# Block inverses of the gated DeltaNet mixer: 32x32 diagonal blocks for four levels, the last level as single 32x32 products

## The chip, the cores and the metric

One NeuronCore of a Trainium2 chip runs the whole layer in one launch. The time is the device time of one execution in microseconds (us), given as the median of several executions. TensorE (PE) multiplies, VectorE (DVE) and ScalarE (ACT) do element-wise work and empty PSUM, GpSimd (POOL) and SyncE (SP) mostly start transfers. A matmul of 32-bit floats shows in the trace as two MATMUL records and two weight loads (LDWEIGHTS, engine PEld), so 16 matmuls are 32 records.

## The reference, cut to what matters

The layer is a half-step SwiGLU network, a token mixer and a second SwiGLU network. Half of the mixer is a gated DeltaNet with 8 heads in both directions, in chunks of 64 tokens. For every chunk it solves a unit lower triangular 64x64 system:

```python
def gdn_chunked(q, k, v, beta, g, h0):
    ...
    kk = jnp.einsum('bhnck,bhnmk->bhncm', k, k)
    a_mat = eye + jnp.where(pos[:, None] > pos[None, :], beta[..., :, None] * decay * kk, 0.0)
    rhs = jnp.concatenate([beta[..., None] * v, (beta * gamma)[..., None] * k], axis=-1)
    sol = lax.linalg.triangular_solve(a_mat, rhs, left_side=True, lower=True, unit_diagonal=True)
    ...
    def step(h, xc):
        u = vt_c - jnp.einsum('bhck,bhkv->bhcv', w_c, h)
        o = jnp.einsum('bhck,bhkv->bhcv', qg_c, h) + jnp.einsum('bhcm,bhmv->bhcv', pqk_c, u)
        h = h * gl_c[..., None, None] + jnp.einsum('bhck,bhcv->bhkv', kd_c, u)
        return h, o
```

The 256 context and 256 latent tokens are 8 chunks per head and direction. The other half of the mixer is a 2-D Fourier transform ("fnet" in the code).

## The kernel before, in words

Before and after the mixer the kernel runs large projections: TensorE multiplies weight tiles that ACT and DVE split into two parts each (`parts`). The change touches none of this.

The mixer is a loop written out by hand, `for i in range(-1, HEADS + 1)`, once for each engine: `mixer_pe`, `mixer_dve`, `mixer_act`. In iteration i three heads are in work: head i+1 (`a`) gets its decays and its chunk matrix, head i (`m`) gets its inverse, head i-1 (`b`) runs its scan over the 8 steps. Every engine executes its instructions in the order written; semaphores (`hs[...]`, counted per head by `PER`) tie the engines together. Iteration 0 also carries the Fourier half.

All 8 chunks of a head stand side by side in one tile of 128 partitions by 512 columns: partitions 0 to 63 hold the forward direction, 64 to 127 the backward one, and each chunk has 64 columns. The inverse S of (I + N) is built by doubling the size of the diagonal blocks, from 2 to 64. `start_S` makes the first S (the 2x2 blocks) out of `n_T` with two DVE instructions, `start_T` transposes it into `g_T`. Each of the five levels is then a chain through two engines:

- PE `y_level`: `n_T` (stationary) times `g_T` (moving), 8 chunks x 2 halves = 16 matmuls into bank B_Y
- DVE `level_Y`: times the mask `LEVEL[lv]`, out to `g_Y`
- PE `x_level`: `g_Y` (stationary) times `g_S` (moving), 16 matmuls into bank B_X
- DVE `level_S`: `g_S` minus the product
- DVE `level_T`: `g_T` is the transpose of `g_S` (not after the last level)

```python
for s in range(STEPS):
    last = pair_mm(B_Y, CHUNK * s, n_T[:, m.h % 2, s, :], g_T[:, m.h % 2, s, :])
```

`pair_mm` issues one 64x64 matmul for the upper and one for the lower partitions. `DVE transpose` works within 32x32 blocks. After level 4 (the fifth) PE runs `solve_w` and `solve_v`, which multiply S with `kbg` and `vb`.

Between the products of the levels stand the scan of head b (`scan_read` s on PE, `scan_u` s on DVE, `scan_write` s on PE, `scan_state` s on DVE, in that circle) and, for head m, transposes of keys and values (`token_k`, `token_v`). ACT is in the loop for `decays` (`dT`), `values` (`vb`), `w_out_of` (`wT`), `vt_out_of` (`vt`) and the output norm. In the last iterations the output projection starts: `split_out` on ACT and DVE and `out_products` on PE.

## Time and profile before

| | |
|---|---|
| median of 3 runs | 3061.83 us (3061.67 to 3066.12) |
| profiled execution, its own time | 3063.91 us |
| its span in the trace | 3062.1 us |
| busy: PE, PEld, DVE, ACT, POOL | 97%, 80%, 59%, 31%, 1% of the span |
| granted TensorE clock, mean | 0.991 |
| mixer loop in the trace | from about 1912 us to about 2226 us |
| from the first level product of head 1 to that of head 7 | 1959.43 to 2160.04 us, six heads |

The profile's page gives shares over the whole span, which the large projections fill. The mixer is a tenth of it; what bounds it has to be read from the timeline of each engine in one head's iteration and from the chain of waits there. A MATMUL's time in a timeline row runs to its modelled end; from the start of one row to the start of the next is the time that the products take in a stream.

### The profile page before, as it was taken

To read this page: it belongs to the slowest core of one execution; us is meant where nothing else is said; L and a number is where in the kernel's file an instruction comes from. 1 tells how busy PE (TensorE), PEld (TensorE's weight loads), DVE (VectorE), ACT (ScalarE), POOL (GpSimd) and SP (SyncE) were. 2 spreads that over 40 slices of the span, in tenths; PEclk is the share of its full clock that TensorE was granted. 3 is DMA by queue.
4 is the path that set the end of the run, shared out by engine and by line. 5 is a ranking of instruction groups with operands and counts; after the bars stand their busy time and mean duration, and the time that the engine had idled before them with its cause. 6 is when DMAs were issued, how large, how long until landed. Compare 5 with 4: busy or idle time off the path is not lost. (4 is left out here: it accounts for less than half of the span.)

```text
span 3062.1 us, 43016 instructions
## 1 busy us (share of the span) xinstructions
PE 2959.7 (97%) x17705; PEld 2444.6 (80%) x17705; DVE 1814.1 (59%) x2027; ACT 949.2 (31%) x1155; POOL 25.3 (1%) x35
## 2 busy tenths in 40 slices
PE   6899999999999999999979999999999999999998
PEld 3688888888888888888868899777777888888887
DVE  3346565665565656565674566667556655666666
ACT  3222221221222222221352356211245343434333
POOL 0000000000000000000000000000000000000000
PEclk9999999999999999999989999999999999999999
DMA  9726444454544557575723354000254555555553
GB/s 370 267 96 206 137 165 152 151 180 136 194 147 155 202 211 261 182 271 202 291 64 105 97 168 141 10 9 9 92 185 165 182 189 192 179 190 179 192 191 124
DMA packets 307694, 508.07 MB, mean 166 GB/s; under 512 B 8252, under 2 KB 230020, under 8 KB 291684
## 3 DMA queue, kind: packets, MB, share of 16 engines
q1 hardware_dynamic: 305312, 496.83, 48.0%
q0 software_dynamic: 1408, 8.86, 0.8%
q8 instruction: 112, 1.84, 0.3%
q10 hardware_dynamic: 836, 0.33, 0.0%
q14 instruction: 26, 0.21, 0.0%
HBM read 503.85 MB, written 2.15 MB: 165 GB/s over the span
## 5 line engine op out<-in xcount | busy, mean ns | idle before, releaser
L2182 PE MATMUL ps<-xn,parts 128*128 128x512 f32 (+1 forms) x8992 | 1788.9, 361 | 6.6 <-DVE parts L1471 3.2
L2182 PEld LDWEIGHTS ps<-xn,parts 128*128 128x128 f32 x8992 | 1515.7, 189 | 277.7 <-issue 6.8
L1471 DVE TENSOR_TENSOR parts<-raw,parts 128x1024 fp32r<-128x1024 f32 x632 | 755.9, 1221 | 412.6 <-ACT parts L828 412.3
L828 ACT ACTIVATE parts<-raw 128x1024 fp32r<-128x1024 f32 x634 | 656.2, 1055 | 1093.3 <-PE ps L2182 890.3
L2182 PE MATMUL ps<-parts,h_parts 128*128 128x512 f32 x3168 | 729.8, 390 | 1.6 <-DVE h_f L1516 1.5
L2182 PEld LDWEIGHTS ps<-parts,h_parts 128*128 128x128 f32 x3168 | 591.5, 188 | 135.5 <-issue 6.1
L1504 DVE SCALAR_TENSOR_TENSOR macc<-raw,cs,macc 128x2048 f32<-128x2048 f32 x150 | 348.1, 2346 | 0.0
L1606 DVE TENSOR_TENSOR acc<-acc,ps 128x512 f32<-128x512 f32 x160 | 110.0, 688 | 212.4 <-PE ps L2182 212.4
L866 ACT ACTIVATE h_parts<-h_f 128x512 fp32r<-128x512 f32 (+1 forms) x42 | 35.1, 836 | 356.2 <-DVE h_f L1563 356.2
L1563 DVE TENSOR_TENSOR h_f<-silu_g,ps 128x1024 f32<-128x1024 f32 x20 | 24.4, 1222 | 146.0 <-PE ps L2182 146.0
L2182 PE MATMUL ps<-parts,xn 128*128 128x512 f32 x384 | 91.6, 394 | 0.0
L2182 PEld LDWEIGHTS ps<-parts,xn 128*128 128x128 f32 x384 | 71.0, 188 | 15.1 <-issue 0.5
L1598 DVE TENSOR_TENSOR acc<-acc,ps 128x1024 f32<-128x1024 f32 x42 | 51.3, 1221 | 35.3 <-PE ps L2182 32.4
L1557 DVE TENSOR_REDUCE h_f<-ps 128x512 f32<-128x1024 f32 x22 | 27.0, 1226 | 73.3 <-PE ps L2182 73.3
L1551 DVE TENSOR_REDUCE silu_g<-ps 128x512 f32<-128x1024 f32 x22 | 27.0, 1226 | 72.3 <-PE ps L2182 72.3
L1796 DVE SCALAR_TENSOR_TENSOR cv<-ps,convT,cv 128x248 f32<-128x248 f32 (+3 forms) x160 | 66.1, 472 | 0.1
L1565 DVE TENSOR_TENSOR h_parts<-h_f,h_parts 128x512 fp32r<-128x512 f32 (+1 forms) x42 | 39.8, 947 | 37.9 <-ACT h_parts L866 37.9
L1896 PE MATMUL ps<-g_T,n_T 64*64 64x64 f32 x1280 | 45.9, 221 | 2.6 <-DVE g_T L1224 1.7
L1896 PEld LDWEIGHTS ps<-g_T,n_T 64*64 64x64 f32 x1280 | 40.4, 134 | 8.2 <-DVE g_T L1224 6.0
L1896 PE MATMUL ps<-g_S,g_Y 64*64 64x64 f32 x1280 | 45.9, 221 | 1.0 <-DVE g_Y L1218 0.2
L1896 PEld LDWEIGHTS ps<-g_S,g_Y 64*64 64x64 f32 x1280 | 40.4, 134 | 7.2 <-DVE g_Y L1218 4.5
L2182 PE MATMUL ps<-raw,cpad 128*32 128x512 f32 x160 | 25.0, 715 | 18.6 <-DMA raw<-in_w_mod 18.6
(239 smaller groups left out, 1205.8 us busy)
## 6 DMA issues: line engine op xcount, KB each, us to landing
raw<-in_w_mod SPq DMA_DIRECT2D x132, 1024.0 KB, 5.4
raw<-in_w_up SPq DMA_DIRECT2D x88, 1024.0 KB, 5.1
raw<-in_w_down SPq DMA_DIRECT2D x88, 1024.0 KB, 5.3
raw<-in_w_gate SPq DMA_DIRECT2D x84, 1024.0 KB, 5.1
raw<-in_w_in SPq DMA_DIRECT2D x41, 1024.0 KB, 5.3
raw<-in_w_out SPq DMA_DIRECT2D x16, 1024.0 KB, 5.1
extra<-in_w_mod SPq DMA_DIRECT2D x12, 1024.0 KB, 14.3
gate_raw<-in_w_gate SPq DMA_DIRECT2D x4, 1024.0 KB, 14.2
```

Of the source, the lines that this page charges most:

```text
L828: nc.scalar.activation(parts[:, unit % PART_SLOTS, 0, :], raw[:, slot, b * UNIT:(b + 1) * UNIT], ACT.Copy).then_inc(hi_ready, 1)
L866: nc.scalar.activation(gpart[:, 0, 2 * s:2 * s + 2, :], h_f32[:, :, 0:N], ACT.Copy).then_inc(h_hi, 1)
L1471: nc.vector.tensor_tensor(parts[:, pslot, 1, :], raw[:, slot, b * UNIT:(b + 1) * UNIT], parts[:, pslot, 0, :].bitcast(F32), ALU.subtract)\
L1504: ins = nc.vector.scalar_tensor_tensor(macc[:, s, :], raw[:, slot, :], cs[:, k, s:s + 1], macc[:, s, :], ALU.mult, ALU.add)
L1551: nc.vector.tensor_reduce(silu_g[:, :, 0:N], halves(4 * s), axis=mybir.AxisListType.X, op=ALU.add).then_inc(g_sum, 1)
L1557: nc.vector.tensor_reduce(h_f32[:, :, 0:N], halves(up), axis=mybir.AxisListType.X, op=ALU.add).then_inc(u_sum, 1)
L1565: nc.vector.tensor_tensor(gpart[:, 1, 2 * s:2 * s + 2, :], h_f32[:, :, 0:N], gpart[:, 0, 2 * s:2 * s + 2, :].bitcast(F32), ALU.subtract)\
L1598: nc.vector.tensor_tensor(a[:, :, cols], a[:, :, cols], ps[:, bank:bank + 2, :], ALU.add).then_inc(down_added, 1)
L1606: nc.vector.tensor_tensor(a[:, t, cols], a[:, t, cols], ps[:, down_bank(tiles, j, t), :], ALU.add).then_inc(down_added, 1)
L1796: nc.vector.scalar_tensor_tensor(o, s_, tap, o, ALU.mult, ALU.add).then_inc(conv_op, 1)
L1896: return nc.tensor.matmul(o, lhsT, rhs, start=start, stop=stop)
L2182: return nc.tensor.matmul(o, lhsT, rhs, start=start, stop=stop)
```

## The change

S is kept compact while its diagonal blocks are at most 32 wide: `c_S` and `c_T` hold 32 columns per chunk (256 in all) where `g_S` and `g_T` held 64 (512 in all). Two ACT instructions per head, `diagonal_blocks`, copy `n_T` into `n_D` and zero the off-diagonal 32x32 blocks by a per-partition scale of 0 or 1 (`SIDE`). `start_S` becomes three DVE instructions of 256 columns. In levels 0 to 3 the products stay 16 matmuls each with the same 64x64 stationary operand, and move 32 columns instead of 64; `level_Y` still writes 512 columns, `level_S` and `level_T` handle 256. `inverse_blocks`, two ACT instructions, spreads `c_S` into the full `g_S` (now one buffer). The last level is built apart: `outer_y` and `outer_x` are 16 matmuls each with a stationary operand of 32x32, ACT copies the product between them (`outer_Y`), and the result goes into `g_S` by one ACT instruction (`outer_forward`) and one DVE instruction (`outer_backward`) on 32 partitions each. The constants shrink from 10 to 8 small masks.

```diff
@@ -232,12 +241,14 @@
...
-        g_T = ra("g_T", [P, 2, STEPS, CHUNK])
-        g_S = ra("g_S", [P, 2, STEPS, CHUNK])
+        c_T = ra("c_T", [P, 2, STEPS, BLOCK])
+        c_S = ra("c_S", [P, 2, STEPS, BLOCK])
+        g_S = ra("g_S", [P, STEPS, CHUNK])
+        g_Y = ra("g_Y", [P, STEPS, CHUNK])
         c2 = sb("c2", [P, C2_COLS], R_RAW + 3 * slot_bytes)
         rp = Bump(R_PARTS, R_PARTS + slot_bytes)
         n_T = rp("n_T", [P, 2, STEPS, CHUNK])
-        g_Y = rp("g_Y", [P, STEPS, CHUNK])
+        n_D = rp("n_D", [P, 2, STEPS, CHUNK])
         rp = Bump(R_PARTS + slot_bytes, R_PARTS + 2 * slot_bytes)
         kbg = rp("kbg", [P, STEPS, P])
         vb = rp("vb", [P, STEPS, P])
@@ -434,14 +454,14 @@
 
         PER = {
 
-            "gm_ok": 1, "e_mm": 1, "e_exp": 1, "kk_mm": 1, "sb_ok": 1, "ib_ok": 1, "n_half": 1, "n_ok": 1,
-            "t_init": 1, "s_half": 1, "s_init": 1,
+            "gm_ok": 1, "e_mm": 1, "e_exp": 1, "kk_mm": 1, "sb_ok": 1, "ib_ok": 1, "n_half": 1, "n_ok": 1, "nd_ok": 2,
+            "t_init": 1, "s_init": 3,
 
             "kT": 2, "kd_ok": 2, "kbg_ok": 2, "vT": 2, "vb_ok": 2, "qg_ok": 1,
             "qk_mm": 1, "p_half": 1, "p_ok": 3, "f_a": 1, "f_mid_ok": 1, "f_b": 1, "f_even": 1, "f_v": 2, "f_hi": 1,
             "f_lo": 1,
 
-            "y_mm": 5, "y_ok": 5, "x_mm": 5, "t_ok": 4, "s_ok": 5, "w_mm": 1, "w_ok": 2, "vt_mm": 2,
+            "y_mm": 5, "y_ok": 5, "x_mm": 5, "t_ok": 4, "s_ok": 4, "S_ok": 4, "w_mm": 1, "w_ok": 2, "vt_mm": 2,
             "vt_ok": 2,
 
             "wh_mm": 7, "u_ok": 7, "dh_mm": 7, "st_ok": 13, "oT_mm": 1, "osq": 1, "oss_mm": 1, "oss_ln": 1,
@@ -689,6 +709,30 @@
                 a.ago(2, "n_half", "p_half")
                 nc.scalar.activation(flat(dT[:, a.h % 2]), ps[:, B_A, :], ACT.Exp).then_inc(hs["e_exp"], 1)
 
+            def diagonal_blocks(a):
+                a.wait("n_ok")
+                a.ago(2, "y_mm", "s_init")
+                for e, cols in enumerate(SIDES):
+                    nc.scalar.activation(n_D[:, a.h % 2, :, cols], n_T[:, a.h % 2, :, cols], ACT.Copy, scale=SIDE[e])\
+                        .then_inc(hs["nd_ok"], 1)
+
+            def inverse_blocks(m):
+                m.wait("s_ok")
+                m.last("vt_mm")
+                for e, cols in enumerate(SIDES):
+                    nc.scalar.activation(g_S[:, :, cols], c_S[:, m.h % 2], ACT.Copy, scale=SIDE[e])\
+                        .then_inc(hs["S_ok"], 1)
+
+            def outer_Y(m):
+                m.wait("y_mm")
+                nc.scalar.activation(y_off, blocks(B_Y), ACT.Copy).then_inc(hs["y_ok"], 1)
+
+            def outer_forward(m):
+                m.wait("x_mm")
+                m.wait("S_ok", 2)
+                nc.scalar.activation(g_S[Q0, :, SIDES[1]], blocks(B_X, Q0), ACT.Copy, scale=-1.0)\
+                    .then_inc(hs["S_ok"], 1)
+
             def values(m, g):
                 m.wait("vT", g + 1)
                 m.last("vt_mm")
@@ -763,6 +807,8 @@
                     out_root(was)
                 if not m and a:
                     fnet_mid(fn[0])
+                if a:
+                    diagonal_blocks(a)
                 if first:
                     fnet_between(1)
                     fnet_between(2)
@@ -785,13 +831,19 @@
                     values(m, 1)
                     if first:
                         fnet_mid(fn[6])
+                    inverse_blocks(m)
+                    outer_Y(m)
+                    if first:
                         fnet_between(6)
+                    if i < HEADS - 1:
+                        outer_forward(m)
                 if i == HEADS - 1:
                     act.wait_ge(hs["qg_ok"], HEADS)
                     act.wait_ge(hs["p_ok"], HEADS * PER["p_ok"])
                     act.wait_ge(hs["e_mm"], HEADS)
                     act.wait_ge(hs["n_ok"], HEADS)
                     split_out(0)
+                    outer_forward(m)
                     split_out(1)
                 if i == HEADS:
                     act.wait_ge(hs["x_mm"], HEADS * PER["x_mm"])
@@ -1192,15 +1244,17 @@
 
             def start_T(a):
                 a.wait("s_init")
-                nc.vector.transpose(flat(g_T[:, a.h % 2]), flat(g_S[:, a.h % 2])).then_inc(hs["t_init"], 1)
+                nc.vector.transpose(flat(c_T[:, a.h % 2]), flat(c_S[:, a.h % 2])).then_inc(hs["t_init"], 1)
 
             def start_S(a):
-                a.wait("n_ok")
+                a.wait("nd_ok")
                 a.ago(2, "vt_mm")
-                S = g_S[:, a.h % 2]
-                nc.vector.tensor_tensor(S, n_T[:, a.h % 2], every(M1T), ALU.mult).then_inc(hs["s_half"], 1)
-                a.wait("s_half")
-                nc.vector.tensor_tensor(S, every(PAIR_ID), S, ALU.subtract).then_inc(hs["s_init"], 1)
+                S, D = c_S[:, a.h % 2], n_D[:, a.h % 2]
+                nc.vector.tensor_tensor(S, D[:, :, SIDES[0]], D[:, :, SIDES[1]], ALU.add).then_inc(hs["s_init"], 1)
+                a.wait("s_init", 1)
+                nc.vector.tensor_tensor(S, S, every(OWN_M1T), ALU.mult).then_inc(hs["s_init"], 1)
+                a.wait("s_init", 2)
+                nc.vector.tensor_tensor(S, every(OWN_ID), S, ALU.subtract).then_inc(hs["s_init"], 1)
 
             def token_k(m, g, part):
                 src = ps[:, (B_A, B_B)[g], :].rearrange("p (s c) -> p s c", s=4)
@@ -1215,13 +1269,16 @@
 
             def level_Y(m, lv):
                 m.wait("y_mm", lv + 1)
-                nc.vector.tensor_tensor(g_Y[:], ps[:, B_Y, :].rearrange("p (s c) -> p s c", c=CHUNK), every(LEVEL[lv]),
+                two = [P, STEPS, 2, BLOCK]
+                nc.vector.tensor_tensor(g_Y[:].rearrange("p s (e c) -> p s e c", e=2),
+                                        blocks(B_Y).unsqueeze(2).to_broadcast(two),
+                                        LEVEL[lv].rearrange("p (e c) -> p e c", e=2).unsqueeze(1).to_broadcast(two),
                                         ALU.mult).then_inc(hs["y_ok"], 1)
 
             def level_T(m, lv):
 
                 m.wait("s_ok", lv + 1)
-                nc.vector.transpose(flat(g_T[:, m.h % 2]), flat(g_S[:, m.h % 2])).then_inc(hs["t_ok"], 1)
+                nc.vector.transpose(flat(c_T[:, m.h % 2]), flat(c_S[:, m.h % 2])).then_inc(hs["t_ok"], 1)
 
             def level_S(m, lv):
                 m.wait("x_mm", lv + 1)
@@ -1229,8 +1286,14 @@
                     m.wait("s_ok", lv)
                 else:
                     m.wait("s_init")
-                S = flat(g_S[:, m.h % 2])
-                nc.vector.tensor_tensor(S, S, ps[:, B_X, :], ALU.subtract).then_inc(hs["s_ok"], 1)
+                S = flat(c_S[:, m.h % 2])
+                nc.vector.tensor_tensor(S, S, ps[:, B_X, 0:STEPS * BLOCK], ALU.subtract).then_inc(hs["s_ok"], 1)
+
+            def outer_backward(m):
+                m.wait("x_mm")
+                m.wait("S_ok", 2)
+                nc.vector.tensor_scalar(g_S[Q3, :, SIDES[0]], blocks(B_X, Q3), -1.0, None, ALU.mult)\
+                    .then_inc(hs["S_ok"], 1)
 
             def query_gates(m):
                 m.eng.wait_ge(gam_in[m.h % 2], 16 * (m.h // 2 + 1))
@@ -1430,7 +1493,6 @@
                 if i == HEADS - 1:
                     query_matrix(m)
 
-                level_Y(m, 4)
                 if b:
                     scan_u(b, 7)
                 if i + 2 < HEADS:
@@ -1438,7 +1500,7 @@
                 if first:
                     fnet_out(fn[6])
                     fnet_lo(fn[6])
-                level_S(m, 4)
+                outer_backward(m)
                 if i < HEADS - 1:
                     query_half(m)
                     query_matrix(m)
@@ -1976,9 +2038,9 @@
                 else:
                     m.wait("t_init")
                     m.last("vt_ok")
-                    m.wait("n_ok")
+                    m.wait("nd_ok")
                 for s in range(STEPS):
-                    last = pair_mm(B_Y, CHUNK * s, n_T[:, m.h % 2, s, :], g_T[:, m.h % 2, s, :])
+                    last = pair_mm(B_Y, BLOCK * s, n_D[:, m.h % 2, s, :], c_T[:, m.h % 2, s, :], BLOCK)
                 inc(last, "y_mm")
 
             def x_level(m, lv):
@@ -1988,19 +2050,37 @@
                 else:
                     m.wait("s_init")
                 for s in range(STEPS):
-                    last = pair_mm(B_X, CHUNK * s, g_Y[:, s, :], g_S[:, m.h % 2, s, :])
+                    last = pair_mm(B_X, BLOCK * s, g_Y[:, s, :], c_S[:, m.h % 2, s, :], BLOCK)
                 inc(last, "x_mm")
 
+            def outer_y(m):
+                m.wait("t_ok")
+                m.wait("y_ok", LEVELS)
+                m.wait("n_ok")
+                for s in range(STEPS):
+                    cols = slice(BLOCK * s, BLOCK * s + BLOCK)
+                    mm(ps[Q1, B_Y, cols], n_T[Q0, m.h % 2, s, SIDES[1]], c_T[Q0, m.h % 2, s, :])
+                    last = mm(ps[Q2, B_Y, cols], n_T[Q3, m.h % 2, s, SIDES[0]], c_T[Q3, m.h % 2, s, :])
+                inc(last, "y_mm")
+
+            def outer_x(m):
+                m.wait("y_ok")
+                m.wait("s_ok")
+                for s in range(STEPS):
+                    cols = slice(BLOCK * s, BLOCK * s + BLOCK)
+                    mm(ps[Q0, B_X, cols], y_off[Q1, s, :], c_S[Q1, m.h % 2, s, :])
+                    last = mm(ps[Q3, B_X, cols], y_off[Q2, s, :], c_S[Q2, m.h % 2, s, :])
+                inc(last, "x_mm")
+
             def solve_w(m):
 
-                m.wait("s_ok")
-                m.wait("t_ok")
+                m.wait("S_ok")
                 m.wait("kbg_ok")
                 for s in range(STEPS):
                     for half, c_ in enumerate((s, high_block(back(s)))):
                         rows = HALVES[half]
                         last = mm(ps[:, B_XT + half, CHUNK * s:CHUNK * s + CHUNK], kbg[rows, c_, :],
-                                  g_S[rows, m.h % 2, c_, :])
+                                  g_S[rows, c_, :])
                 inc(last, "w_mm")
 
             def solve_v(m, g):
@@ -2156,13 +2236,13 @@
                 if b:
                     scan_write(b, 6)
 
-                y_level(m, 4)
+                outer_y(m)
                 if b:
                     scan_read(b, 7)
                 if first:
                     fnet_positions(fn[6])
                     fnet_channels(fn[7])
-                x_level(m, 4)
+                outer_x(m)
                 if b:
                     scan_write(b, 7)
                 if first:
```

On DVE, in the iteration of a middle head, from the second level on, the order before is (g_Y, g_S, g_T are `level_Y`, `level_S`, `level_T`; u_buf and st the scan):

```order
849 L1288 SCALAR_TENSOR_TENSOR st<-st,sc_all,ps 128x128 x2
850 L1233 TENSOR_TENSOR g_S<-g_S,ps 128x512
851 L1277 TENSOR_TENSOR u_buf<-vt,ps 128x128
852 L1224 STREAM_TRANSPOSE g_T<-g_S 128x512
853 L1288 SCALAR_TENSOR_TENSOR st<-st,sc_all,ps 128x128 x2
854 L1300 TENSOR_TENSOR o_out<-o_out,qzf 128x256
855 L1218 TENSOR_TENSOR g_Y<-ps,c_108 128x512
856 L1277 TENSOR_TENSOR u_buf<-vt,ps 128x128
857 L1201 TENSOR_TENSOR g_S<-n_T,early 128x512
858 L1203 TENSOR_TENSOR g_S<-early,g_S 128x512
859 L1233 TENSOR_TENSOR g_S<-g_S,ps 128x512
```

and now:

```order
850 L1351 SCALAR_TENSOR_TENSOR st<-st,sc_all,ps 128x128 x2
851 L1290 TENSOR_TENSOR c_S<-c_S,ps 128x256
852 L1340 TENSOR_TENSOR u_buf<-vt,ps 128x128
853 L1281 STREAM_TRANSPOSE c_T<-c_S 128x256
854 L1351 SCALAR_TENSOR_TENSOR st<-st,sc_all,ps 128x128 x2
855 L1363 TENSOR_TENSOR o_out<-o_out,qzf 128x256
856 L1273 TENSOR_TENSOR g_Y<-ps,c_110 128x512
857 L1340 TENSOR_TENSOR u_buf<-vt,ps 128x128
858 L1253 TENSOR_TENSOR c_S<-n_D 128x256
859 L1255 TENSOR_TENSOR c_S<-c_S,early 128x256
860 L1257 TENSOR_TENSOR c_S<-early,c_S 128x256
861 L1290 TENSOR_TENSOR c_S<-c_S,ps 128x256
```

The order is the same but for the third instruction of `start_S`; the subtractions and transposes have half the columns, the masked copies to g_Y have not.

On ACT, one middle head before:

```order
448 L690 ACTIVATE dT<-ps 128x512
449 L733 ACTIVATE r_o<-ps,ssq 128x256
450 L736 ACTIVATE r_o<-r_o 128x256
451 L740 ACTIVATE xn_52<-o_out 128x256
452 L695 ACTIVATE vb<-ps 128x512 x2
453 L728 ACTIVATE sq_o<-ps 128x256
454 L716 ACTIVATE wT<-ps 128x8x64 x2
```

and now:

```order
458 L710 ACTIVATE dT<-ps 128x512
459 L777 ACTIVATE r_o<-ps,ssq 128x256
460 L780 ACTIVATE r_o<-r_o 128x256
461 L716 ACTIVATE n_D<-n_T,early 128x8x32 x2
462 L784 ACTIVATE xn_52<-o_out 128x256
463 L739 ACTIVATE vb<-ps 128x512 x2
464 L723 ACTIVATE g_S<-c_S,early 128x8x32 x2
465 L728 ACTIVATE g_Y<-ps 128x256
466 L733 ACTIVATE g_S<-ps 32x8x32
467 L772 ACTIVATE sq_o<-ps 128x256
468 L760 ACTIVATE wT<-ps 128x8x64 x2
```

Six instructions per head are new on ACT, all in the order in which their inputs come.

## Rows read from the trace of the kernel before

**Rows 1.** The page: busy time by engine over the whole span.
```profile
PE 2959.7 (97%) x17705; PEld 2444.6 (80%) x17705; DVE 1814.1 (59%) x2027; ACT 949.2 (31%) x1155; POOL 25.3 (1%) x35
```

**Rows 2.** Windows: busy time in the two parts of head 3's iteration.
```profile
core 0: us, PE busy (x) PEld busy (x) DVE busy (x) ACT busy (x) POOL busy (x), PEclk, DMA share, GB/s
2026.77:2042.44 15.67, 13.52 (x254) 10.38 (x252) 14.62 (x33) 0.96 (x3) 1.04 (x1) 1.00 0.01 2
2042.44:2060.42 17.98, 17.98 (x298) 14.61 (x298) 8.69 (x21) 4.70 (x10) 0.61 (x1) 1.00 0.06 16
```

**Rows 3.** Chain of waits, same stretch: start us, us, what.
```profile
2042.44 5.01 PE ps L1896 x86
...
2047.78 7.07 PE ps L1896 x127
```

**Rows 4.** Timeline of PE, first part: start, us, form, records [idle before <- releaser].
```profile
2032.41 1.15 PE L1896 MATMUL ps<-g_T,n_T 64*64 64x64 f32 x32 [0.18 <-DVE g_T L1224]
...
2036.52 0.49 PE L1896 MATMUL ps<-u_buf,kd 64*128 64x128 f32 x4 [0.62 <-DVE u_buf L1277]
2037.14 1.15 PE L1896 MATMUL ps<-g_T,n_T 64*64 64x64 f32 x32
...
2042.44 0.44 PE L1896 MATMUL ps<-st,wT 128*64 128x128 f32 x4 [0.58 <-DVE st L1288]
```

**Rows 5.** Timeline of DVE, both parts.
```profile
2035.58 0.69 DVE L1233 TENSOR_TENSOR g_S<-g_S,ps 128x512 f32<-128x512 f32 x1 [0.65 <-PE ps L1896]
...
2036.38 0.70 DVE L1224 STREAM_TRANSPOSE g_T<-g_S 128x512 f32<-128x512 f32 x1
...
2038.34 0.69 DVE L1218 TENSOR_TENSOR g_Y<-ps,c 128x512 f32<-128x512 f32 x1 [0.34 <-PE ps L1896]
...
2039.14 0.68 DVE L1201 TENSOR_TENSOR g_S<-n_T,early 128x512 f32<-128x512 f32 x1
...
2049.20 0.61 DVE L1288 SCALAR_TENSOR_TENSOR st<-st,sc_all,ps 128x128 f32<-128x128 f32 x2 [1.16 <-PE ps L1896]
...
2053.59 0.42 DVE L1246 TENSOR_TENSOR p_h<-dT,ps 128x256 f32<-128x256 f32 x1 [0.58 <-PE ps L1896]
```

**Rows 6.** Timeline of PE, second part, from the last level on.
```profile
2049.09 1.15 PE L1896 MATMUL ps<-g_T,n_T 64*64 64x64 f32 x32
2050.16 0.44 PE L1896 MATMUL ps<-st,wT 128*64 128x128 f32 x4
2050.53 0.66 PE L1896 MATMUL ps<-qg,st 128*128 128x64 f32 x4
2051.12 1.15 PE L1896 MATMUL ps<-g_S,g_Y 64*64 64x64 f32 x32
2052.20 0.66 PE L1896 MATMUL ps<-pT,u_buf 128*128 128x64 f32 x4
...
2053.40 2.00 PE L1896 MATMUL ps<-g_S,kbg 64*128 64x64 f32 x32
...
2055.96 1.96 PE L1896 MATMUL ps<-vb,g_S 64*64 64x128 f32 x32
```

**Rows 7.** Timeline of ACT, second part.
```profile
2048.19 0.60 ACT L695 ACTIVATE vb<-ps 128x512 f32<-128x512 f32 x1 [5.69 <-PE ps L1896]
2052.89 0.38 ACT L728 ACTIVATE sq_o<-ps 128x256 f32<-128x256 f32 x1 [4.11 <-PE ps L1896]
```

**Rows 8.** Timeline of PE in head 0, where the Fourier products stand between.
```profile
1935.27 1.15 PE L1896 MATMUL ps<-g_T,n_T 64*64 64x64 f32 x32 [0.45 <-DVE g_T L1224]
...
1946.19 1.15 PE L1896 MATMUL ps<-g_T,n_T 64*64 64x64 f32 x32
1947.44 1.16 PE L1896 MATMUL ps<-c,f_mid 128*128 128x129 f32 x8
```

**Rows 9.** Timeline of PE at the gates: matmuls on 32 rows, 32 moving columns.
```profile
1790.14 0.30 PE L1883 MATMUL ps<-c,gate_buf 32*64 32x32 f32 x4
1790.38 0.36 PE L1880 MATMUL ps<-c,gate_buf 32*128 32x32 f32 x3
```

More of the change, by code:

```diff
@@ L35 @@
 LSTEPS = SEQ // CHUNK
+BLOCK = 32
+LEVELS = 4
 ROW = 64
@@ L84 @@
 N_FULL = 4
-N_PAIR = 10
-N_EARLY = 5
+N_PAIR = 8
+N_EARLY = 4
 C2_COLS = (N_PAIR - N_EARLY) * CHUNK + 2 * P + 4 * SEQ
@@ L127, in level, with pair, own @@
         return strict & (m // (2 * s) == i // (2 * s)) & (m // s != i // s)
-    small = [np.eye(P), incl, strict.T, level(1), level(1).T] + [level(s) for s in (2, 4, 8, 16, 32)]
-    masks += [np.concatenate([x[:CHUNK, :CHUNK], x[CHUNK:, CHUNK:]], 0) for x in small]
+    def pair(x):
+        return np.concatenate([x[:CHUNK, :CHUNK], x[CHUNK:, CHUNK:]], 0)
+    def own(x):
+        return np.concatenate([x[b:b + BLOCK, b:b + BLOCK] for b in range(0, P, BLOCK)], 0)
+    sides = np.stack([np.arange(P) // BLOCK % 2 == e for e in range(2)], 1)
+    masks += [np.concatenate([own(np.eye(P)), own(level(1).T)], 1), pair(incl), pair(strict.T),
+              np.repeat(sides, BLOCK, axis=1)]
+    masks += [pair(level(s)) for s in (2, 4, 8, 16)]
     t = np.arange(SEQ)
@@ L269, in build_layer @@
         early = sb("early", [P, N_EARLY, CHUNK], R_LATE + 4 * P)
-        PAIR_ID, P_INCL, P_LATER, _, M1T = (early[:, n, :] for n in range(N_EARLY))
-        LEVEL = [c2[:, n * CHUNK:(n + 1) * CHUNK] for n in range(N_PAIR - N_EARLY)]
+        P_INCL, P_LATER = early[:, 1, :], early[:, 2, :]
+        OWN_ID, OWN_M1T = early[:, 0, 0:BLOCK], early[:, 0, BLOCK:CHUNK]
+        SIDE = [early[:, 3, BLOCK * e:BLOCK * e + 1] for e in range(2)]
+        SIDES = [slice(BLOCK * e, BLOCK * e + BLOCK) for e in range(2)]
+        Q0, Q1, Q2, Q3 = (slice(BLOCK * q, BLOCK * q + BLOCK) for q in range(4))
+        LEVEL = [c2[:, n * CHUNK:(n + 1) * CHUNK] for n in range(LEVELS)]
+        y_off = g_Y[:].rearrange("p s c -> p (s c)")[:, 0:STEPS * BLOCK].rearrange("p (s c) -> p s c", c=BLOCK)
         cv = sb("cv", [P, 4, TOK], R_QZ + 8192)
@@ L388, in build_layer, with blocks @@
         B_Y, B_XT, B_X, B_A, B_B, B_S0, B_S1, B_O = range(8)
+        def blocks(bank, rows=slice(0, P)):
+            return ps[rows, bank, 0:STEPS * BLOCK].rearrange("p (s c) -> p s c", c=BLOCK)
         def halves(bank):
@@ L1182, in chunk_half @@
                 a.wait("kk_mm")
-                a.ago(2, "y_mm", "s_half")
+                a.ago(2, "y_mm", "nd_ok")
                 nc.vector.tensor_tensor(flat(n_T[:, a.h % 2]), flat(dT[:, a.h % 2]), ps[:, B_B, :], ALU.mult)\
@@ L2014, in solve_v @@
                         last = mm(ps[rows, (B_Y, B_XT)[g], P * (s % 4):P * (s % 4) + P],
-                                  g_S[rows, m.h % 2, c_, :], vb[rows, c_, :])
+                                  g_S[rows, c_, :], vb[rows, c_, :])
                 inc(last, "vt_mm")
```

## The prediction

> **What bounds the kernel now.** The page comes first: over the span PE is busy 97% and DVE 59% [rows 1]. That is an average over the large projections, which the change leaves alone, so it says only that time won in the mixer is not given back to an idle engine later. What it is worth in the mixer is read from one head. The windows cut head 3's iteration at the points where the releaser changes: a first part of 15.67 us, in which DVE is busy 14.62 and PE 13.52, and a second of 17.98 us, in which PE is busy all 17.98 and DVE 8.69; ACT has 0.96 and 4.70 [rows 2]. Six heads (1 to 6) run at this period of 33.65 us. The chain of waits says the same: from 2042.44 on it lies on PE without a break, in pieces such as 5.01 and 7.07 us [rows 3]; before that it hops between DVE and PE. The PE timeline shows what PE waits for in the first part: the transpose `g_T`, `u_buf` of the scan (0.62), and `st` (0.58) [rows 4]. The DVE timeline shows why these are late: they stand behind the 512-column subtraction (0.69) and transpose (0.70) of the level on DVE's queue, and DVE itself waits only 0.65 and 0.34 for PE [rows 5]. So in the first part shorter DVE instructions count, in the second shorter PE products.
>
> **First part: DVE instructions of half the columns.** A DVE instruction of 128x512 takes 0.69, one of 128x256 (`p_h`, with an input in PSUM as here) 0.42 [rows 5]: `level_S` gains 0.27. No transpose of 256 columns is in the trace; it is bounded by nothing gained (0.70) and by the half (0.35), and I take the same ratio as above, 0.43, a gain of 0.27. `level_Y` still writes 512 columns and gains nothing. `start_S` was two instructions of about 0.69 and is three of about 0.42: nothing, too (0.1 at best). Walking through the first part:
> - level 0: S and T gain 0.54, and the second Y product, which waited 0.18 for `g_T` [rows 4], starts 0.54 earlier.
> - level 1: Y product, copy, X product, S, `u_buf`, T follow each other with hardly a gap (2032.41 to 2037.14, [rows 4]). 0.54 more, so 1.1.
> - level 2: 0.54 more on DVE. PE then waited 0.58 for `st` at 2042.44 [rows 4], and `st` is behind S and T. The wait goes, and so 1.1 + 0.6 = 1.7.
>
> Is there room on PE? It was busy 13.52 of 15.67 us [rows 2], and a busy time includes the ends of products that a follower could overlap; 15.67 - 1.7 = 13.97 still holds it. **1.7 us per head.**
>
> **Levels 0 to 3 on PE: half the moving columns.** Here lies the question. Three rows of 32 records each tell what a product costs: stationary 64x64 with 64 moving columns 1.15 us; stationary 64x128 with 64 moving 2.00; stationary 64x64 with 128 moving 1.96 [rows 6]. Doubling either side doubles the time, so the two run beside each other and the longer sets the pace; at 64 and 64 both are at the limit. If only the moving side is halved, the stationary side still sets the pace. The product of 128 stationary and 64 moving columns with all rows in use says so too: 4 records of `qg` take from 2050.53 to 2051.12, 0.15 us each, as long as the weights ask for although few columns move [rows 6]. I take 1.15 to 1.10 us (only the last record's end gets shorter); the other end is the half, 0.55. The Trainium skill, "TensorEngine Tiling (Array Packing)", section "Instruction Overhead", speaks against this part of the change as well: a matmul has about 60 cycles of overhead, and one column has the latency of 60. By it 64 to 32 columns would bring nothing; the trace agrees in so far as no shorter product stands in it. Gain in the second part, two such products: 0.05.
>
> **The last level on PE.** `outer_y` and `outer_x` have 32 stationary and 32 moving columns. From 128 to 64 the longer side took a product from 2.00 to 1.15, 0.85 for 64 columns; 32 fewer again give 1.15 - 0.43 = 0.7, an estimate. Its bounds are 0.55 (the half) and 1.9: at the gates 4 records on 32 rows take from 1790.14 to 1790.38, 0.06 each [rows 9], times 32; that row is one chain of weights without a second tile beside it. I take 0.7, as the Y products also run two tiles side by side. What follows in the second part:
> - `outer_y` gains 0.43, but the next on PE is `scan_read` 7, which needs `st` 6: DVE has it at 2049.20 + 0.61 = 2049.81, and the read stood at 2050.16 [rows 5, 6]. So 0.3 counts and a wait of 0.1 appears.
> - `outer_x` waits for ACT's copy `outer_Y`. An ACT instruction of 256 columns takes 0.38 [rows 7]; `scan_read` 7 with `qg` covers it (2050.16 to 2051.12, [rows 6]). It costs nothing; without this cover it would cost 0.5. Gain 0.43, whole.
> - `solve_w` needs four ACT and DVE pieces of `g_S`. `outer_forward` and `outer_backward` (about 0.4, side by side) lie beside `pT` and `qk` products, 1.2 us (2052.20 to 2053.40, [rows 6]). Nothing.
>
> Together **0.3 + 0.43 + 0.05 = 0.8 us per head.**
>
> **What is added on ACT**, six instructions, about 2.3 us, to an engine busy 5.66 of 33.65 us [rows 2]. `diagonal_blocks` stands right behind `r_o` and is needed by `start_S` some 10 us later (2039.14, [rows 5]). `inverse_blocks` is queued behind `vb` (2048.19 + 0.60, [rows 7]) and takes until about 2049.6; the product for `outer_Y` is done at about 2049.8. Behind them wait `sq_o` and `wT`, whose products end later. Nothing on the path, with 0.2 to 0.4 to spare.
>
> **The sum.** Heads 1 to 6: 6 x (1.7 + 0.8) = 15.0. Head 7 has no next head on DVE but the same waits: 2.5. Head 0 is filled by Fourier products: the one DVE wait of 0.45 goes, and 0.4 for one outer product; behind the other stands a product that waits for its own ACT copy (1946.19 + 1.07 is before 1947.44) [rows 8]: 0.8. The prologue gets one ACT step more before `start_S`, hidden behind Fourier products on PE: 0. Total 18.3. After the mixer PE is the bound, and all moves up. 3063.91 - 18.3 = 3045.6; the profiled execution stood 2.1 above the median, so **3043.5 us**. Of that saving 10.2 + 1.7 comes from DVE and only about 6 from PE, though the diff halves PE's columns.
>
> **Rivals.**
> - *The moving columns set the pace.* Then a level product costs 0.55. In the second part 2 x 0.5 = 1.0 more per head; in the first at most another 1.0, as DVE (14.62 - 1.7 of 14.0 us) is the bound there. 8 x 2.0 = 16 more: 3027.5. For it: Y and solve_v differ by the moving side alone. Against: solve_w.
> - *The gain is eaten in the last level.* The products of 32x32 cost 1.9 each and not 0.7: 1.2 more each, 2.4 a head and 19 in all, so 3062.5, no change. For it: [rows 9], the only row with 32 rows and 32 columns. Against: it has a single row group.
> - *Slower: two 32x32 tiles do not run side by side at all.* Each record would then run to its own end before the next starts: 4 of them take 0.30 to their end at the gates, with starts 0.06 apart, so at least 0.30 - 3 x 0.06 = 0.12 each [rows 9]. 32 x 0.12 = 3.8 per product, 3.1 over the forecast, 6.2 per head, 50 in all: 3093.5. It decides from where the two products eat 2.3 us per head, at 1.85 each. Place: `outer_y`, whose two tiles write one PSUM bank. The Trainium skill, same page, "Gotcha 1: PSUM Pressure", says that different row tiles cannot access the same bank simultaneously; by it this would be the outcome. The trace disagrees for tiles of 64 rows: the Y product writes both halves into one bank in 1.15 us, and solve_w, with two banks, is no faster per column [rows 6].
>
> **How the numbers follow.** Forecast 0.77, first rival 0.12, no change 0.07, slower 0.04. Own range of the forecast: transposes at 0.35 and all of the outer gain give 3037; transposes that gain nothing (8 x 3 x 0.27 = 6.5) and an ACT hand-over that shows (0.3 per head) give 3052.5. With part of the first rival: 3033 to 3053. About 0.2% (6 us) is what a measurement of this kernel can tell from no change. Faster by over 0.2%: 0.89; within: 0.07; slower: 0.04.
>
> **What would show it.** The windows of a head: the first part 14.0 us, the second 17.2, the period 31.15. PE's level products at 1.10, outer ones at 0.7. DVE `c_S` 0.42, `c_T` 0.43. The wait for `st` at `scan_read` 5 gone, a new one of 0.1 at `scan_read` 7. Wrong would be: level products near 0.55, outer products at 1.9 or more, PE waiting for ACT at `outer_x` or `solve_w`, or a transpose of 256 columns at 0.7.

## The result, and the profile after

| | before | changed |
|---|---|---|
| median | 3062.34 us (3059.88 to 3066.12, 11 runs) | 3074.76 us (3064.03 to 3093.59, 11 runs) |
| ratio | | 1.0038, 95% interval 1.0025 to 1.0051 |
| span of the profiled execution | 3062.1 us | 3073.0 us |
| mean granted clock in it | 0.991 | 0.979 |

The change makes the kernel slower by 0.4%, where 0.6% faster was forecast. The scatter is new, too: 6 us before, 30 us now. The mean granted clock lies between 0.972 and 0.983 in the 11 runs of the changed kernel, so every one of them lost clock, not the profiled one alone; the slowest has the lowest. The page of the changed kernel, busy time by engine and the line of the granted clock in 40 slices, already has the cause in it:

```profile
PE 2980.0 (97%) x17705; PEld 2463.5 (80%) x17705; DVE 1788.0 (58%) x2027; ACT 968.4 (32%) x1203; POOL 24.4 (1%) x35
...
PEclk9999999999999999999989999997799999999999
```

The same number of PE instructions as before [rows 1] is busy 20 us longer, although many of them move fewer columns; and in two slices in the mixer the clock stands at 7 tenths, where before every slice from the 26th on had 9 or more. The windows of the changed kernel give the places. First comes head 3 cut at the same points as in [rows 2], then head 5 cut where the clock changes, then head 7 with the start of the tail:

```profile
core 0: us, PE busy (x) PEld busy (x) DVE busy (x) ACT busy (x) POOL busy (x), PEclk, DMA share, GB/s
2021.29:2035.34 14.05, 13.22 (x253) 10.37 (x251) 12.97 (x34) 1.34 (x4) 1.04 (x1) 1.00 0.01 2
2035.34:2052.51 17.17, 17.09 (x299) 13.76 (x298) 7.18 (x20) 6.78 (x14) 0.61 (x1) 1.00 0.07 18
2083.71:2093.40 9.69, 8.86 (x178) 6.86 (x177) 8.83 (x22) 0.93 (x3) 1.04 (x1) 1.00 0.02 3
2093.40:2127.50 34.10, 34.10 (x343) 28.16 (x340) 11.52 (x31) 5.82 (x12) 0.61 (x1) 0.50 0.04 9
...
2159.39:2203.00 43.61, 42.17 (x512) 34.90 (x510) 19.54 (x47) 8.07 (x16) 0.59 (x1) 0.61 0.14 50
```

At full clock a head takes 14.05 + 17.17 = 31.22 us (33.65 before, 31.15 forecast). In head 5 the granted clock falls to 0.50, which is the lower of TensorE's two levels, 1.2 instead of 2.4 GHz, 9.7 us after the head's first Y product, and stays there for 34.1 us. Such a stretch is called a fall below. (Stretches at 0.50 outside the heads stand in both kernels, for instance at the start of the mixer: the clock from 1880 to 1920 us is 0.91 before and after.) The head takes from 2083.71 to 2129.51, 45.8 us instead of 31.2: 14.6 us lost. The second fall begins 9.0 us into head 7. From head 7's first Y product to the end of the program the changed kernel takes 3073.0 - 2159.39 = 913.6 us, and a later run of almost the same kernel without such a fall (`first_wide` below) 3043.7 - 2145.02 = 898.7: 14.9 us more. Take both off and 3073.0 becomes 3043.5; the forecast of the span was 3062.1 - 18.3 = 3043.8.

In the PE timeline of the changed kernel the same products stand at the two clocks (start, us, form, records):

```profile
2027.77 0.49 PE L1958 MATMUL ps<-u_buf,kd 64*128 64x128 f32 x4 [0.23 <-DVE u_buf L1340]
...
2030.25 0.49 PE L1958 MATMUL ps<-u_buf,kd 64*128 64x128 f32 x4 [0.39 <-DVE u_buf L1340]
...
2036.30 1.12 PE L1958 MATMUL ps<-c_T,n_D 64*64 64x32 f32 x32
...
2041.94 0.69 PE L1958 MATMUL ps<-c_T,n_T 32*32 32x32 f32 x32
2042.71 0.44 PE L1958 MATMUL ps<-st,wT 128*64 128x128 f32 x4
...
2043.66 0.69 PE L1958 MATMUL ps<-c_S,g_Y 32*32 32x32 f32 x32
...
2102.47 1.92 PE L1958 MATMUL ps<-c_T,n_D 64*64 64x32 f32 x32
...
2112.33 1.06 PE L1958 MATMUL ps<-c_T,n_T 32*32 32x32 f32 x32
...
2118.09 3.68 PE L1958 MATMUL ps<-g_S,kbg 64*128 64x64 f32 x32
```

A level product with half the moving columns takes 1.12 us where it took 1.15 [rows 6], an outer one 0.69; at the lower level 1.92 and 1.06. `solve_w`, which the change does not touch, goes from 2.00 [rows 6] to 3.68. What does not run on TensorE keeps its time. The DVE timeline of head 3 after the change, the counterpart of [rows 5], and as its last line the subtraction inside the fall of head 5, 0.42 us as at full clock:

```profile
2029.54 0.42 DVE L1290 TENSOR_TENSOR c_S<-c_S,ps 128x256 f32<-128x256 f32 x1 [0.63 <-PE ps L1958]
...
2030.11 0.44 DVE L1281 STREAM_TRANSPOSE c_T<-c_S 128x256 f32<-128x256 f32 x1
...
2042.05 0.61 DVE L1351 SCALAR_TENSOR_TENSOR st<-st,sc_all,ps 128x128 f32<-128x128 f32 x2 [1.65 <-PE ps L1958]
...
2098.40 0.42 DVE L1290 TENSOR_TENSOR c_S<-c_S,ps 128x256 f32<-128x256 f32 x1 [1.36 <-PE ps L1958]
```

and of ACT, where the new instructions lie beside the scan:

```profile
2041.54 0.90 ACT L723 ACTIVATE g_S<-c_S,early 128x256 f32<-128x256 f32 x2
2042.68 0.38 ACT L728 ACTIVATE g_Y<-ps 128x256 f32<-128x256 f32 x1 [0.24 <-PE ps L1958]
2044.40 0.37 ACT L733 ACTIVATE g_S<-ps 32x256 f32<-32x256 f32 x1 [1.34 <-PE ps L1958]
```

So every price in the sum came out, and the sum did not. What is left to explain is why the clock falls, and which part of the change does it. It is not idleness: in the stretch before the fall PE is busy 8.86 of 9.69 us (91%) and waits nowhere longer than 0.39 us. In the same 9.69 us of a head of the kernel before it is busy 8.31 (86%), with the wait of 0.62 of [rows 4] at the end, and there the clock held:

```profile
core 0: us, PE busy (x) PEld busy (x) DVE busy (x) ACT busy (x) POOL busy (x), PEclk, DMA share, GB/s
2026.77:2036.46 9.69, 8.31 (x164) 6.25 (x162) 9.04 (x21) 0.01 (x1) 1.04 (x1) 1.00 0.01 2
```

The Trainium skill, "TensorE: Matmul & The Clock Gate", Part 1, says that a gate sets the clock by how busy TensorE has been, and advises against idle gaps. Idle gaps are not what these rows show before the fall: the kernel with the longer waits kept the clock.

### The profile page after: what moved, and what is told of

Same layout as the page of the kernel before. It is cut to its first block and busy times, and to the rows that moved or that the text cites. A ratio compares the mean times of both kernels' runs of the same rounds, so it can differ in the third digit from the quotient of the medians.

```text
span 3073.0 us, 43085 instructions
## 1 busy us (share of the span) xinstructions
PE 2980.0 (97%) x17705; PEld 2463.5 (80%) x17705; DVE 1788.0 (58%) x2027; ACT 968.4 (32%) x1203; POOL 24.4 (1%) x35
## 5 line engine op out<-in xcount | busy, mean ns | idle before, releaser
L1958 PEld LDWEIGHTS ps<-c_S,g_Y 64*64 64x64 f32 (+1 forms) x1280 | 40.8, 140 | 7.3 <-DVE g_Y L1273 4.1
L1958 PE MATMUL ps<-c_S,g_Y 64*64 64x32 f32 (+1 forms) x1280 | 45.4, 224 | 0.8
L1351 DVE SCALAR_TENSOR_TENSOR st<-st,sc_all,ps 128x128 f32<-128x128 f32 x96 | 28.8, 341 | 28.2 <-PE ps L1958 27.5
L2262 PE MATMUL ps<-raw,cpad 128*32 128x512 f32 x160 | 25.0, 715 | 18.3 <-DMA raw<-in_w_mod 18.3
L1094 ACT ACTIVATE cv<-ps,convT 128x512 f32<-128x512 f32 (+1 forms) x24 | 13.5, 612 | 91.4 <-PE ps L2262 91.4
```

The source lines that it names most:

```text
L1351: nc.vector.scalar_tensor_tensor(st[:, d, :], st[:, d, :], sc_all[:, K_LASTF + d, b.h, c_:c_ + 1], ps[:, B_S0 + d, 0:P], ALU.mult, ALU.add ...
L1958: return nc.tensor.matmul(o, lhsT, rhs, start=start, stop=stop)
L2262: return nc.tensor.matmul(o, lhsT, rhs, start=start, stop=stop)
```

## The experiments

Theory A: the falls come from the moved columns, which the change halves in the level products, in 8 of 10 at nearly unchanged duration, since the stationary operand sets their pace. Rivals: B, the 32x32 tiles of the last level; C, the zero blocks in `n_D`, or the denser heads as such. The first four ran on one chip.

### inner_wide: the moved columns back in levels 0 to 3

The moving operand is read twice, so that 64 columns move; nothing else is gained or lost by it.

```diff
+            def twice_mm(bank, s, lhsT, rhs):
+
+                o = ps[:, bank, CHUNK * s:CHUNK * s + CHUNK].rearrange("p (e c) -> p e c", e=2)
+                for rows in HALVES:
+                    last = mm(o[rows], lhsT[rows], rhs[rows].unsqueeze(1).to_broadcast([CHUNK, 2, BLOCK]))
+                return last
...
-                    last = pair_mm(B_Y, BLOCK * s, n_D[:, m.h % 2, s, :], c_T[:, m.h % 2, s, :], BLOCK)
+                    last = twice_mm(B_Y, s, n_D[:, m.h % 2, s, :], c_T[:, m.h % 2, s, :])
```

The X products are written in the same way; `level_Y` reads all 512 columns again, `level_S` the first 32 of each 64.

> The changed kernel with the moving operand of the Y and X products in levels 0 to 3 read twice (64 moving columns again, the second 32 a copy of the first); the last level stays 32x32 with 32 columns. The heads at full clock took 31.2 us as forecast, and the loss came with two stretches of 34 us at granted clock 0.5. Theory A (the clock fell because TensorE moves fewer columns per time): the mean granted clock is 0.991 as before, no stretch of the heads is at 0.5, head period 31.3 us, about 3045. Theory B (the clock fell because of the 32x32 tiles of the last level): falls stay, clock 0.972 to 0.983, 3064 to 3093. Theory C (it has to do with the blocks of zeros in n_D, or with the denser heads): falls stay too.

Measured: 3054.72 us (3047.41 to 3056.61, 6 runs), ratio to before 0.997 (0.9957 to 0.9982). The profiled execution took 3047.41 with a clock of 0.99 and no fall in the heads. The 20 us less than in the changed kernel come from columns whose results nobody reads. The 32x32 tiles, the zeros in `n_D` and the dense heads are all still there, so B and C fall as causes by themselves. Four of the six runs, though, lay above 3054.

### all_wide: the last level too

The products of `outer_y` and `outer_x` get the same doubled moving operand.

> As inner_wide, and the two products of the last level move 64 columns too (stationary 32x32). Theory A: clock 0.991, no falls; outer products 1.1 us where they took 0.69, so the head is up to 0.5 us longer than in inner_wide, 31.3 to 31.8, about 3045 to 3049. Theory B and C: falls as in the changed kernel, 3064 to 3093.

Measured: 3051.16 us (3050.54 to 3053.28, 5 runs), ratio 0.9961 (0.9947 to 0.9976), clock 0.991. The outer products take 1.08 us each where they took 0.69 with 32 moving columns, so behind a stationary operand of 32 columns the moving side does set the time. The scatter is gone:

```profile
2037.86 1.15 PE L1956 MATMUL ps<-c_T,n_D 64*64 64x64 f32 x32
...
2043.55 1.08 PE L1956 MATMUL ps<-c_T,n_T 32*32 32x64 f32 x32
...
2045.52 1.08 PE L1956 MATMUL ps<-c_S,g_Y 32*32 32x64 f32 x32
```

Its head takes 31.98 us, the windows say. This separates the two terms of the forecast, as PE here moves 64 columns in every product of the levels: of 33.65 - 31.98 = 1.67 us nearly all is due to DVE, whose instructions are shorter and, in the last level, fewer (forecast 1.7); the outer products at 1.08 instead of 1.15 can hold 0.14 of it at most. inner_wide's 31.35 adds 0.63 for the two small outer products (forecast 0.7), the changed kernel's 31.22 the last 0.13 (forecast 0.05).

### outer_wide: the last level alone

> The changed kernel with 64 moving columns in the last level alone; levels 0 to 3 move 32. Theory A: only 2 of 10 products are back at 64 columns, so falls stay or become a little rarer, 3055 to 3090. Theory B in the form that the columns of the last level decide: no falls, clock 0.991, 3045 to 3049.

Measured: 3088.23 us (3079.86 to 3098.09, 4 runs), ratio 1.0092 (1.0064 to 1.012). Two falls, of 34.1 us each, stand in the trace; the first of them in the windows of outer_wide, from the head's first Y product on:

```profile
core 0: us, PE busy (x) PEld busy (x) DVE busy (x) ACT busy (x) POOL busy (x), PEclk, DMA share, GB/s
2022.08:2031.00 8.92, 8.13 (x164) 6.25 (x162) 8.30 (x21) 0.91 (x3) 1.04 (x1) 1.00 0.01 2
2031.00:2065.10 34.10, 34.06 (x332) 28.55 (x334) 12.04 (x32) 4.62 (x10) 0.61 (x1) 0.50 0.04 9
```

Columns added in the last level did not help; the interval is even above that of the changed kernel (1.0025 to 1.0051). Its head at full clock is 31.86 us, 0.64 longer, which makes 5 of the 13 us between the two; the rest is open. The falls stayed, as theory A allowed, but did not become rarer, and it is the first sign that the place of the columns matters.

### before_half: the narrowing alone, in the kernel before

```diff
-                    last = pair_mm(B_Y, CHUNK * s, n_T[:, m.h % 2, s, :], g_T[:, m.h % 2, s, :])
+                    wd = CHUNK if lv == 4 else 32
+                    last = pair_mm(B_Y, CHUNK * s, n_T[:, m.h % 2, s, :], g_T[:, m.h % 2, s, 0:wd], wd)
```

The X products are cut in the same way; DVE's instructions keep their 512 columns.

> The kernel before with one thing changed: in levels 0 to 3 the Y and X products move only the first 32 of the 64 columns; DVE reads these 32 twice, so its instructions keep 512 columns. The inverses are computed wrongly by this: the second half of the columns is left out. No 32x32 tiles, no n_D, heads as slow as before. Theory A: the clock falls in the mixer, mean below 0.991, the time above 3062 by up to 30 us. Theory B and C: clock 0.991, 3060 to 3062, since the products shrink by 0.03 us each.

Measured: 3158.33 us (3146.11 to 3162.26, 4 runs), ratio 1.0314 (1.0297 to 1.0331), clock 0.958. One cut in the moved columns, which saves 0.03 us a product, costs 95 us. The trace has seven falls, one in each of heads 1 to 7. Its windows from the first Y product of head 3 to the fall, and through it (head 4 begins at 2096.14):

```profile
core 0: us, PE busy (x) PEld busy (x) DVE busy (x) ACT busy (x) POOL busy (x), PEclk, DMA share, GB/s
2051.84:2061.70 9.86, 8.34 (x166) 6.39 (x166) 9.23 (x21) 0.01 (x1) 1.05 (x1) 1.00 0.01 2
2061.70:2089.00 27.30, 27.30 (x282) 22.78 (x282) 13.06 (x28) 1.99 (x4) 0.00 (x0) 0.50 0.04 11
```

With no small tiles, no `n_D` and no new ACT instructions, A stands and B and C are excluded as necessary parts. Before the fall PE is busy 8.34 of 9.86 us (85%), which is the share of the kernel before (86% in its first 9.69 us), so busy time does not part these two either. I had expected 30 us at most. Why this kernel has seven falls and the changed one two is open: the old DVE instructions make PE wait longer here, and so somewhat fewer columns move in the same time, but no run tests whether that is the reason.

### y_wide, inner_wide_2, all_wide_2, outer_y_wide: doses

These four ran together. y_wide restores the Y products of levels 0 to 3 only, outer_y_wide is inner_wide with a doubled moving operand in `outer_y` only, which TensorE can afford since it waits for `st` behind it.

> The changed kernel with the Y products alone of levels 0 to 3 at 64 moving columns; X products and the last level at 32. A dose between the changed kernel and inner_wide. Theory A: fewer or shorter falls than in the changed kernel (3064 to 3094) and more than in inner_wide (3047 to 3057): 3050 to 3070.

> inner_wide again, on the same chip as the other three. Its earlier runs lay between 3047.4 and 3056.6; one stretch of half clock in the heads would explain the upper ones. Theory A: most runs 3054 to 3057 with a lower mean clock, a few at 3047.

> all_wide again, on the same chip: 3050.5 to 3053.3 and no fall of the clock, so slower than a run of inner_wide without a fall and faster than one with it.

> As inner_wide, and of the last level only outer_y moves 64 columns; outer_x stays at 32. In all_wide the head was 31.98 us against 31.35 in inner_wide; of this 0.63, outer_y should cost little, since TensorE waits for st behind it anyway. If the moved columns decide (theory A), 9 of 10 products at full width leave falls of the clock rare: head 31.5 us, 3047 to 3050, narrower spread than inner_wide. If not, the spread is that of inner_wide, 3047 to 3057.

| | products with 64 columns, of 10 | median (range), us | ratio (interval) | falls in the profiled heads |
|---|---|---|---|---|
| y_wide | 4 | 3057.65 (3047.29 to 3060.36, 5 runs) | 0.9974 (0.9961 to 0.9987) | one, of 34.1 us |
| inner_wide_2 | 8 | 3053.62 (3045.72 to 3056.92, 6 runs) | 0.9963 (0.9951 to 0.9975) | two, of 10.2 and 6.8 us |
| outer_y_wide | 9 | 3048.16 (3044.16 to 3050.2, 5 runs) | 0.9946 (0.9933 to 0.9959) | none |
| all_wide_2 | 10 | 3051.51 (3049.1 to 3053.56, 5 runs) | 0.9958 (0.9945 to 0.997) | none |

The more of the products are wide, the less time the profiled heads spend at the lower level: 68.2 us in the changed kernel, then 34.1, 17.0 and none. The last product of the ten costs more than it brings: the head goes from 31.60 to 31.98 us, and neither profiled run has a fall. What a short fall is worth shows in inner_wide_2, whose profiled execution had two. Its windows, a head at full clock, then the next up to the fall and the fall:

```profile
core 0: us, PE busy (x) PEld busy (x) DVE busy (x) ACT busy (x) POOL busy (x), PEclk, DMA share, GB/s
2019.17:2050.52 31.35, 30.52 (x550) 24.13 (x548) 20.19 (x53) 8.10 (x18) 1.66 (x2) 1.00 0.04 11
2050.52:2074.10 23.58, 22.75 (x430) 18.01 (x428) 18.61 (x48) 4.03 (x10) 1.04 (x1) 1.00 0.05 14
2074.10:2084.30 10.20, 10.20 (x85) 8.86 (x85) 1.44 (x5) 2.50 (x6) 0.61 (x1) 0.50 0.01 2
```

The head with 10.2 us at the lower level took from 2050.52 to 2086.58, 36.06 us, 4.7 more than its neighbour. The second fall lasted 6.8 us. One or two such falls have the size of the step between the lower runs of inner_wide (3045.7 to 3049) and the upper (3052 to 3057); the runs without a profile give their time and mean clock alone, and the clock agrees: 0.989 to 0.990 in the four lower runs, 0.987 to 0.988 in the eight upper ones. This fall began 23.6 us into the head, not 9, so the first part is not the only weak place once it is filled.

### narrow_extra: columns at the head's end

```diff
-                inc(mm(ps[:, B_A, :], STRICT, flat(gm[:, a.h % 2])), "e_mm")
+                for n in range(3):
+                    last = mm(ps[:, B_A, :], STRICT, flat(gm[:, a.h % 2]))
+                inc(last, "e_mm")
```

> The changed kernel with its narrow products as they are, and one product of the decays (stationary 128x128, 512 moving columns) issued three times for each head instead of once, into the same bank and with the same values. It adds 1024 columns on all 128 rows per head; the narrowing took 10 products x 16 matmuls x 32 columns on 64 rows or fewer. At full clock a head costs 2.1 us more (1.07 each), 33.3 us. Theory A1 (what counts is the sum of moved columns over some time, wherever they come from): the falls become rare or go, 3058 to 3064. Theory A2 (narrow instructions as such bring the clock down while they run): falls as in the changed kernel on top of the 17 us, 3080 to 3110.

Measured: 3120.97 us (3113.74 to 3136.53, 4 runs), ratio 1.0204 (1.017 to 1.0238), clock 0.969. Of the 58 us over before, the added work explains 17 less the 18 that the change should gain, that is nothing. The trace has four falls, of 30.7 to 34.1 us; the one in head 1, in the windows from its first Y product:

```profile
core 0: us, PE busy (x) PEld busy (x) DVE busy (x) ACT busy (x) POOL busy (x), PEclk, DMA share, GB/s
1963.97:1973.90 9.93, 9.04 (x186) 7.05 (x184) 8.86 (x22) 0.91 (x2) 1.04 (x1) 1.00 0.01 2
1973.90:2004.60 30.70, 30.70 (x318) 25.63 (x316) 10.67 (x28) 4.22 (x9) 0.61 (x1) 0.50 0.10 10
```

The sum over a head is not it (A1 falls). Either narrow instructions as such bring the clock down (A2), or the columns must be moved where they are lacking, in the first part (A3). The next three, on one chip, tell these apart.

### first_wide, second_wide, narrow_fill: the place

first_wide has the doubled operand for `lv < 3`, second_wide for `lv == 3` and the last level. narrow_fill leaves every product narrow and adds two others before `scan_write` 2 and 3, in the first part:

```diff
+            def fill():
+                mm(ps[:, B_XT, :], ident, c2[:, C_DFT:C_DFT + 4 * P])
...
                 if b:
+                    fill()
                     scan_write(b, 2)
...
                 if b:
+                    fill()
                     scan_write(b, 3)
```

> The changed kernel with 64 moving columns in the products of levels 0 to 2 alone, which lie in the first part of a head; level 3 and the last level stay at 32. In the traces with falls the clock drops 9 to 10 us after a head's first Y product, at the end of that part, and 1024 added columns at the head's end (narrow_extra) did not help. Theory A3 (the columns moved within the first part decide): near inner_wide, 3045 to 3057, at most short falls. Theory of the sum over a head: with 6 of 10 products back, falls between y_wide and inner_wide too, so this run alone does not exclude it; second_wide does.

> The counterpart: 64 moving columns in level 3 and the last level, levels 0 to 2 at 32. Theory A3: falls as in the changed kernel or outer_wide, 3065 to 3098. Theory of the sum over a head: with 4 of 10 products back as in y_wide, 3047 to 3062.

> The changed kernel, all products narrow, with two products added per head in the first part, where TensorE waits for u_buf anyway (before scan_write 2 and 3): identity 128x128 times 512 columns of constants into a bank that is free then. They change no result. 1.07 us each less the waits of 0.23 and 0.39: about 1.5 us per head, 11 in all. Theory A3: 1024 columns in the right place keep the clock up: no fall in the heads, 3055 to 3060. Theory A2 (narrow instructions as such bring it down): falls as in the changed kernel, 3075 and more.

| | median (range), us | ratio (interval) | falls in the profiled heads |
|---|---|---|---|
| first_wide | 3045.9 (3045.32 to 3053.59, 4 runs) | 0.9953 (0.9936 to 0.997) | none |
| second_wide | 3073.09 (3071.69 to 3084.61, 5 runs) | 1.0043 (1.0027 to 1.0059) | four, of 13.7 us |
| narrow_fill | 3052.93 (3051.37 to 3053.88, 6 runs) | 0.9968 (0.9955 to 0.998) | none |

In second_wide, head 3 in windows to the fall, through it, and to head 4:

```profile
core 0: us, PE busy (x) PEld busy (x) DVE busy (x) ACT busy (x) POOL busy (x), PEclk, DMA share, GB/s
2021.12:2030.30 9.18, 8.35 (x168) 6.47 (x166) 8.55 (x21) 0.92 (x3) 1.04 (x1) 1.00 0.01 2
2030.30:2044.00 13.70, 13.70 (x145) 11.34 (x145) 6.89 (x19) 1.01 (x2) 0.00 (x0) 0.50 0.08 20
2044.00:2058.66 14.66, 14.66 (x247) 11.82 (x244) 4.98 (x15) 6.17 (x13) 0.61 (x1) 1.00 0.01 3
```

The clock falls in heads 3 to 6, always at the same place (9.2 us into the head), and comes back sooner than in the changed kernel (13.7 us against 34.1). Four products restored in the second part give 3073, four restored across both (y_wide) 3058, six in the first part 3046. PE's waits are not what first_wide changes: in its first 9.69 us PE is busy 8.94 us, where it was 8.86 in the changed kernel before the fall, and the clock holds:

```profile
core 0: us, PE busy (x) PEld busy (x) DVE busy (x) ACT busy (x) POOL busy (x), PEclk, DMA share, GB/s
2021.16:2030.85 9.69, 8.94 (x176) 6.84 (x176) 8.80 (x22) 0.92 (x3) 1.04 (x1) 1.00 0.01 2
```

And narrow_fill's PE timeline, where the identity products fill what were waits of 0.23 and 0.39 us:

```profile
2028.51 1.12 PE L1958 MATMUL ps<-c,c 128*128 128x512 f32 x2
2029.57 0.49 PE L1958 MATMUL ps<-u_buf,kd 64*128 64x128 f32 x4
2029.99 1.12 PE L1958 MATMUL ps<-c_S,g_Y 64*64 64x32 f32 x32
...
2031.41 1.13 PE L1958 MATMUL ps<-c,c 128*128 128x512 f32 x2
```

Its head is 32.38 us long, 1.2 more than the changed kernel's, and the kernel is 22 us faster than it: two wide products in the first part kept the clock, though every product of the change stays narrow. So A2 falls. The same two products' worth of columns at the head's end made it slower by 46. A3, that the place decides, stands by second_wide against y_wide, which restore four products each (ratios 1.0043 and 0.9974, intervals apart), and by first_wide. narrow_fill by itself shows less, since it adds columns and closes PE's waits at once (busy 9.60 us of its head's first 9.69, against 8.86). Nor is the plain sum of columns the whole of it: added up over the matmul records of a head's first 9.4 us, y_wide moves about 11,300 columns in head 7, where the clock then fell, and narrow_fill about 10,000, with no fall. The fills use all 128 rows, the level products 64 at a time; which of these differences counts, no run tells.

## Why the prediction was wrong, point by point

- **First part, DVE instructions of half the columns: right.** Subtraction 0.42 (0.42 taken), transpose 0.44 (0.43), three instructions in `start_S` that cost nothing. The part took 14.05 us, 1.62 less than before (14.0 and 1.7 forecast), and all_wide's head is 1.67 shorter.
- **Levels 0 to 3 on PE: the duration was right** (1.12, forecast 1.10), and the first rival (0.55 per product) did not occur. The reading behind it, that the stationary side sets the pace, is also what makes the change harmful: the columns go and the time stays. The prediction books this part as a gain of 0.05 us per head and nothing else; taking it back (inner_wide) makes the changed kernel 20 us faster.
- **The last level: right.** 0.69 against 0.7; `scan_read` 7 now waits for `st`, which DVE has at 2042.05 + 0.61: it starts 0.77 us after `outer_y`, where the next product starts 0.63 after `outer_x`, so the wait is 0.14 (0.1 forecast). The second part took 17.17, 17.2 forecast. The records of the two 32x32 tiles start 0.02 us apart (0.63 / 32), although both write one bank, so they run side by side and the slower rival (0.12 each) did not occur.
- **ACT: right.** `outer_Y` waited 0.24 for PE and not the other way round, and the copy was ready at 2043.06, before `outer_x` at 2043.66.
- **The sum: its terms held (3043.5 for the span without the two falls, 3043.8 forecast); its premise failed.** The step "After the mixer PE is the bound, and all moves up", and with it every duration in the sum, assumed that the clock of [rows 2] (PEclk 1.00) would be granted after the change too. No term and no rival asked what the change does to it. The step that failed is this one: the clock was taken as given, a term of nothing for which no reason stands there. Two falls cost 14.6 + 14.9 = 29.5 us in the profiled execution, against a gain of 18.6. That the terms add up so closely is in part luck: a head gained 2.4 and not 2.5, and from head 7 to the end the program gained 3.4 (902.1 to 898.7) and not 2.5. One reading was wrong without harm to the sum: the period of 33.65 holds for heads 1 to 5, not for six heads, as head 6 took 32.32 us (2127.72 to 2160.04).
- **The rivals: the one that happened was missing.** The rival on the slow side was built on the overlap of tiles. Nothing in the trace of before told that the clock would go, as it is 1.00 there in every window of the heads; but the forecast itself had eight products of a head move half the columns in nearly the same time, and that was reason enough to ask.
- **What would show it** named durations and waits alone. It should have named PEclk in the windows of the heads.
